# Sample attention in four 32-column groups, keys and values in one request, raw tiles without a gate

## The reference, cut to what matters

```python
def nsa_sample(pt, p, slopes, kv_pool, l, page_table, win_buf):
    ...
    raw = kv_pool[l, page_table, :, 0:2].reshape(B, past, 2, G, D)
    ...
    kc = compress(raw[:, :, :, 0], p, 0)          # gelu(blocks of 32 rows @ phi_w1 + b1) @ phi_w2
    vc = compress(raw[:, :, :, 1], p, 1)
    o_cmp, p_cmp = cmp_attend(q, kc, vc, qpos, slopes)
    idx, valid = select_blocks(p_cmp, qpos, total) # the 16 best blocks of 64 keys
    ...
    o_slc = jax.vmap(sel_attend_item, ...)(q, kb, vb, kpos, valid, qpos, slopes)
    ...
    o_win = band_attend(q[:, None], kw[:, None], vw[:, None], qpos[None], kpos_w, slopes)[:, 0]
    y = nsa_merge(pt, o_cmp, o_slc, o_win)
```

## Time and profile before

| | |
|---|---|
| median of 3 runs | 1739.01 us (1738.19 to 1742.09) |
| the profiled execution | 1731.13 us |
| its span, first to last instruction | 1729.0 us |
| TensorE busy | 1400.6 us, 81% |
| VectorE, ScalarE, GpSimd busy | 42%, 28%, 14% |
| DMA, mean | 123 GB/s |
| K/V requests `kv` | 512 of 64 KB, median 2.5 us to landing |
| window requests `rw` | 8 of 512 KB, 4.3 us |
| raw requests `rawc` and `ring` | 128 + 112 of 128 KB from GpSimd, 16 from SyncE |

### The profile page before, as it was taken

One profiled execution on the slowest core, in us unless ns is written; L12 is line 12 of the kernel. 1 busy time (PEld: TensorE's weight loads), 2 busy tenths in 40 slices (PEclk: granted clock), 3 DMA queues, 4 the chain that ended last, 5 costly groups with the idle time before them and its releaser, 6 DMA issues. The chain is left out here.

```text
span 1729.0 us, 23641 instructions
## 1 busy us (share of the span) xinstructions
PE 1400.6 (81%) x7435; PEld 1013.8 (59%) x7435; DVE 721.8 (42%) x1899; ACT 482.8 (28%) x1078; POOL 240.6 (14%) x365
## 2 busy tenths in 40 slices
PE   6899941774699478999999996797988639999991
PEld 4799940343566355677666763497878424455440
DVE  4634445443466225545565444256504621111115
ACT  2000023310155246545565452100320211111112
POOL 1000002000100242244332400000000031111112
PEclk9899985585599768999999988689987869999996
DMA  5234357102000584676566733211132536556524
GB/s 161 49 85 85 78 187 300 40 1 90 0 2 1 124 201 100 152 184 156 142 157 149 165 85 91 81 49 49 62 134 80 207 117 246 218 212 242 200 91 161
DMA packets 210114, 213.33 MB, mean 123 GB/s; under 512 B 82232, under 2 KB 179496, under 8 KB 203144
## 3 DMA queue, kind: packets, MB, share of 16 engines
q1 hardware_dynamic: 185192, 150.25, 29.1%
q0 software_dynamic: 24832, 61.94, 12.4%
HBM read 215.16 MB, written 39.37 MB: 147 GB/s over the span
## 5 line engine op out<-in xcount | busy, mean ns | idle before, releaser
L2664 PE MATMUL bank<-wgu,memtok 128*128 128x512 f32 x384 | 170.4, 597 | 1.8 <-DVE memtok L2867 1.8
L1865 ACT ACTIVATE ZTs<-bank 64x256 f32<-64x256 f32 x320 | 120.6, 377 | 86.3 <-PE bank L1724 82.2
L2664 PEld LDWEIGHTS bank<-wgu,memtok 128*128 128x128 f32 x384 | 73.5, 192 | 94.0 <-issue 94.0
L1227 PE MATMUL bank<-ZTs,w1s 128*128 128x256 f32 x512 | 114.5, 385 | 6.3 <-ACT ZTs L1865 6.3
L1227 PEld LDWEIGHTS bank<-ZTs,w1s 128*128 128x128 f32 x512 | 98.0, 193 | 26.3 <-ACT ZTs L1865 13.0
L1657 DVE COPY ZTs<-bank 64x256 f32<-64x256 f32 x192 | 80.6, 420 | 62.4 <-PE bank L1724 60.3
L1599 POOL DMA_DIRECT2D rawc<-in_cache_nsa_kv x128 | 75.2, 588 | 212.0 <-PE bank L1778 189.0
L257 PE MATMUL bank<-h_high,w_low 128*128 128x272 f32 x384 | 82.0, 295 | 9.1 <-DVE h_low L367 5.1
L2686 PE MATMUL bank<-wdn,yT 128*128 128x512 f32 x192 | 86.5, 593 | 1.5 <-DVE yT L2872 0.9
L1778 PE MATMUL bank<-KTb,QB 128*32 128x512 f32 x144 | 76.5, 615 | 6.6 <-ACT KTb L1894 5.9
L257 PE MATMUL bank<-h_high,w_high 128*128 128x272 f32 x384 | 80.9, 293 | 0.0
(11 more groups left out here) (564 smaller groups left out, 2622.0 us busy)
## 6 DMA issues: line engine op xcount, KB each, us to landing
kv<-in_cache_nsa_kv SPq DMA_DIRECT2D x512, 64.0 KB, 2.5
wgu<-in_exp_w_gate SPq DMA_DIRECT2D x24, 1024.0 KB, 5.0
wgu<-in_exp_w_up SPq DMA_DIRECT2D x24, 1024.0 KB, 7.2
wdn<-in_exp_w_down SPq DMA_DIRECT2D x24, 1024.0 KB, 4.9
rawc<-in_cache_nsa_kv POOLq DMA_DIRECT2D x128, 128.0 KB, 4.2
ring<-in_cache_nsa_kv POOLq DMA_DIRECT2D x112, 128.0 KB, 4.5
rows_dram<-ring POOLq DMA_DIRECT2D x24, 512.0 KB, 12.7
ring<-in_w_in SPq DMA_DIRECT2D x44, 256.0 KB, 3.3
```

The source lines that it names most:

```text
L1227: mm = pe.matmul(dst[:, 2 * nblk * kv:2 * nblk * (kv + 1)], w1[kv][:, c, :], ZT[:, kv, c, :, :].rearrange("p g n -> p (g n)"), start=(c == ...
L1865: return act.activation(dst, src, ACT.Copy)
L2664: mm = pe.matmul(gemm_big[n % 2][:, :].rearrange("p (m f) -> p m f", m=2), XT[:, n % 2, k, :], w[:, :, k, :], start=(k == 0), stop=(k == K ...
```

## The change

The 32 query rows used to fill 32 of the 128 rows of a bank, and 32 of the 128 columns of TensorE. Now four matmuls stand in a row whose results go to rows 0, 32, 64 and 96 (`group(j)`), each with a quarter of the keys or of the value rows. What follows from it:

- `KTb` holds four times 512 keys. Scores are taken in three places of a sequence instead of nine: the window after the first keys (4 x 128 columns), half of the past after step 5, the rest after step 8 (4 x 512 columns each).
- The tables `past`, `masked` and `bwin`, the scores `ss` and `sw` have 128 rows and a quarter of the columns. The mask is added to the table ahead (`mask_table`), and VectorE takes sum and maximum of each half in one instruction.
- Each group has its own maximum; `parts` and `scales` bring the four together, and the fold in `turn_out` (a matmul with the table `fold`) adds the four partial outputs.
- The probabilities are turned by 12 transposes of 128 x 128 or less instead of 39; two of the three banks are copied by VectorE, the last by ScalarE.
- The hidden layer is cut in two halves around the transposes of the probabilities.
- K and V of a block come in one request of 128 KB (`load_kv`), after the values of the sequence before have been taken from the block. The condition on the scores in GpSimd's requests is gone.

```diff
-            KTb = t7("KTb", [P, 2, 512])
-            PTs, PT0 = t7("PTs", [P, 2, 8 * R]), t7("PT0", [P, 3 * R])
+            KTb = t7("KTb", [P, 4, 512])
+            PTs, PT0 = t7("PTs", [P, 2, 512]), t7("PT0", [P, 7 * R])
...
-                return range(AHEAD + 3 * n // 2, AHEAD + 3 * (n + 1) // 2)
+                return range(AHEAD + 12 * (n - 2) // 7, AHEAD + 12 * (n - 1) // 7)
...
-                        for j in range(CT):
-                            sp.wait_ge(kt_mm, b * NKT + (j // 2 + 1))
-                            load_one(j, page, 0, k_here[j // 2])
...
+                    def load_kv(b):
+                        page = page_numbers(SP, b, 0) + page_numbers(SP, b, CT // 2)
+                        sp.wait_ge(o_mm, b * NO + 1)
+                        sp.dma_start(rw[:, :, :, :], I["state_nsa_win"][0, bass.ds(b, 1)].rearrange(
+                            "b (c p) v g d -> p (b c) v (g d)", p=P)).then_inc(rw_here, 16)
+                        for j in range(CT):
+                            sp.wait_ge(o_mm, b * NO + (2 + j // 4))
+                            for half in range(2):
+                                page_half(sp, kv[:, j, :, :, :], page[2 * j + half], half, slice(2, 4)).then_inc(kv_here[j // 2], 16)
...
-                        load_raw(pool, POOL, lambda j: rawc_here[j], b + 2, early, b * CT + CT, b * NKT + NKT)
+                        load_raw(pool, POOL, lambda j: rawc_here[j], b + 2, early, b * CT + CT)
...
+                    def scores(b, h):
+                        pe.wait_ge(kt_out, b * NKT + 5 + 4 * h)
+                        if h:
+                            pe.wait_ge(sl_out, b * 3 + 1)
+                        for j in range(4):
+                            mm = pe.matmul(gemm_big[h][group(j), :], QB[:, b, :], KTb[:, j, :], start=True, stop=True)
+                        mm.then_inc(sl_mm, 1)
...
+                    def values(b, h, u):
...
+                        for a in range(2):
+                            for j in range(4):
+                                at = P * (2 * u + a) + R * j
+                                mm = pe.matmul(o_at(0, group(j)), PTs[:, h, at:at + R], kv[:, 8 * h + 4 * u + j, a, 1, :],
+                                               start=(h + u + a == 0 and j > 0), stop=(h + u + a == 3))
                         mm.then_inc(o_mm, 1)
...
+                        window_scores(b)
+                        for n in range(2, NKT):
+                            keys(b, n)
+                            if more:
+                                turn_raw(b + 1, with_step(n))
+                            if n == 3 and b:
+                                turn_out(b - 1)
+                            if n == 5:
+                                scores(b, 0)
+                        scores(b, 1)
                         if more:
-                            hide(b + 1)
...
+                            hide(b + 1, 0)
+                        turn_new(b)
                         turn(b, 0)
                         turn(b, 1)
...
+                        if more:
+                            hide(b + 1, 1)
+                        values_new(b)
+                        values(b, 0, 0)
                         if more:
                             compressed_keys(b + 1)
+                        values(b, 0, 1)
+                        turn_raw(b + 2, ahead[0:1])
                         if more:
                             compressed_scores(b + 1)
+                        values(b, 1, 0)
+                        turn_raw(b + 2, ahead[1:2])
+                        values(b, 1, 1)
                         if more:
                             importance(b + 1)
+                        turn_raw(b + 2, ahead[2:4])
                         if more:
                             keys(b + 1, 0)
                             keys(b + 1, 1)
```

More of the change, by code:

```diff
@@ new lines, in turn, with values_new @@
+                    def turn(b, h):
+                        bank_ = (work[1], gemm_big[0])[h]
+                        for i in range(4):
+                            mm = pe.transpose(bank_[:, P * i:P * i + P], ss[:, h, P * i:P * i + P], ident)
+                        mm.then_inc(pt_mm, 1)
+                    def values_new(b):
+                        pe.wait_ge(pt_out, b * 2 + 1)
+                        for i in range(4):
+                            pe.matmul(o_at(1, group(i)), PT0[:, R * i:R * i + R], rw[:, i, 1, :],
+                                      start=True, stop=(i > 0))
+                        pe.matmul(o_at(1, group(0)), PT0[0:TS, P + 2 * R:P + 3 * R], vnew[:, 1, :],
+                                  start=False, stop=True)
+                        pe.matmul(o_at(2, group(0)), PT0[:, P:P + R], vc[:, :], start=True, stop=True)
+                        pe.matmul(o_at(0, group(0)), PT0[0:TS, P + R:P + 2 * R], vnew[:, 0, :],
+                                  start=True, stop=False).then_inc(o_mm, 1)
@@ new lines, in parts @@
+                    def parts(b):
+                        dve.wait_ge(e_ready, b * 2 + 2)
+                        c.step(dve.tensor_tensor(gm[0:R, 6:8], gm[0:R, 6:8], st[:, 6:8], ALU.add))
+                        for j in range(4):
+                            ins = dve.tensor_copy(pile[:, j, :], gm[group(j), 4:8])
+                        c.step(ins)
+                        c.step(dve.tensor_reduce(pile2[:, 0:2], pile[:, :, 0:2].rearrange("p j s -> p s j"), AX, ALU.max))
+                        dve.tensor_tensor(part[:, :, :], pile[:, :, 0:2],
+                                          pile2[:, 0:2].unsqueeze(1).to_broadcast([R, 4, 2]), ALU.subtract)\
+                            .then_inc(part_sub, 1)
@@ L2049, in _ @@
-                        dve.tensor_scalar(st[:, 4:5], st[:, 13:14], -1.0, None, ALU.mult).then_inc(m_ready, 1)
-                        scales(b)
+                        ahead = range(AHEAD) if b + 2 < NB else ()
+                        window_out(b)
+                        for n in range(2, NKT):
+                            if more:
+                                copy_z(dve.tensor_copy, dve, b + 1, with_step(n), 1)
+                            if n == 2 and b:
+                                merge(b - 1)
+                            if n == 3:
+                                mask_table()
+                            if n == 5:
+                                if b:
+                                    place(b - 1)
+                                scores_out(b, 0)
@@ L2051, in _ @@
+                        scores_out(b, 1)
+                        maxima(b)
+                        parts(b)
                         turned(b, 0)
                         turned(b, 1)
-                        turned(b, 2)
+                        scales(b)
                         if more:
                             compressed_scores(b + 1)
-                        turned(b, 3)
-                        turned(b, 4)
-                        if b + 2 < NB:
-                            copy_z(dve.tensor_copy, dve, b + 2, range(AHEAD), 1)
@@ L2060, in _ @@
-                        if more:
                             normalize(b + 1)
-                        turned(b, 5)
+                        copy_z(dve.tensor_copy, dve, b + 2, ahead, 1)
                         if more:
```

345 lines of the change are left out of this document (158 added, 187 removed).

## The result

The changed kernel takes 1679.11 us (median of 4 runs, 1676.70 to 1689.35) against 1740.0 for the kernel before on the same chip: a ratio of 0.966, 95% interval 0.962 to 0.970. The forecast was 1723 with a range of 1688 to 1762, so the kernel is 44 us faster than forecast, and outside the range. The profiled execution took 1676.7 us with a span of 1674.7 (before 1731.13 and 1729.0); it was the fastest of the four.

A forecast was written before the change was run, and what follows sets the result against it. TensorE's order was taken as the bound. First sequence to 702, six periods (339 us) to 1041, last period and tail to 1086, against 1101.8 before: -16 us, so 1715 profiled and 1723 as median, range 1688 to 1762.

The forecast's parts named there:

- What bounded the kernel before: Sample attention: TensorE's order was the bound, busy 52.56 of 54.3 us a sequence, with SyncE close behind at 47.7.
- TensorE's work and the column groups: Scores and values: four column groups cost one matmul; 23.9 us removed, 6.9 added, net -17 us a sequence.
- (a) SyncE: Key and value requests: 32 a sequence instead of 64, 0.72 us each, about 23 us, so SyncE stops being a bound.
- (b) DMA: Transfers up to the last keys: 8.0 MB at 250 GB/s take 32 us, so the last keys turn at about 33.
- the zero: The end of a sequence's window values, from which the forecast counted each period.
- Six periods: 6 x 56.5: Steady sequences: six periods of 56.5 us each against 54.3 before, 339 us in all, reaching 1041.
- The clock: Keys' stretch at half clock, 18.5 us or 20 with waits; 2.0 us more in the first half of the hidden layer.
- First sequence: From the first score at 658.2, 20 + 4.7 + 9 + 8.5 + 1.2 us, so its window values end at 702.
- Last sequence and tail: Last period without raw tiles or hidden layer 38.5 us, to 1079.5; value steps, merge and turn 6 us, to 1086.
- Rival 2: Keys' stretch: the clock stays at 1.0, periods of 51 us, end at 1040, -62 us, 1677; chance 0.13.
- Rival 1: K/V loading between values and next keys binds at 225 GB/s: periods of 62 us, 1756; chance 0.29.
- Rival 3: Scores and values: column groups run one behind the other, some +15 us a period, 1816; chance 0.06.

The follow-up runs named there:

- e5: The kernel before with only the gate (raw requests waiting for the scores) removed: 1736.47 us.
- e3: The changed kernel with keys and values asked for apart again, 64 requests of 64 KB a sequence: 1727.08 us.
- e4: The changed kernel with all scores and values in one row group, so no matmuls run side by side: 1727.1 us.
- e2: The changed kernel with one more 512-wide matmul, its result unused, behind each of the seven key groups of a sequence: 1692.85 us.
- e7: The changed kernel with window values and the first two value groups moved ahead of the second hidden half: 1656.01 us, ratio 0.952.
- e8: The changed kernel with half the raw bytes, in as many requests, from the third sequence on: 1661.84 us.
- e1: The changed kernel with GpSimd's first raw tile of the next but one sequence waiting for all scores again: 1697.49 us.
- e6: The kernel before with keys and values in one request, asked for after the values: 1742.39 us, ratio 1.001.

## Why the prediction was wrong, step by step

**What bounded the kernel before: half right.** TensorE's order set the five middle intervals, and removing the gate alone changed nothing (e5). But the prediction put SyncE at 47.7 us a sequence. It had left out the 11.0 us between the sequences, and with them SyncE's cycle is 59 to 61 us. So "TensorE's order is the bound" does not hold for the last two sequences: column groups alone took 8.3 us off the stage (e3), not seven times some 17. The sum of the forecast does not rest on this, since it builds the changed kernel up from its own terms.

**TensorE's work and the column groups: right.** A group of four costs one matmul, 1.07 us against 1.05, and 3.62 when it is made serial (e4). The Trainium skill (TensorE: Matmul & The Clock Gate, Part 3) has three column tiles at 2.38 times the rate of one. By that rule a group of four would cost visibly more than one matmul. No run has three; for four the trace does not agree: from start to start a group takes 0.99 us (666.75 to 667.74, full clock) against 0.98 for one matmul. Busy time in a middle sequence fell from 52.56 to 43.17 us, not by 17; in the last full period, at full clock throughout, it was 37.17, so 15.4 less, and most of the difference is matmuls at half clock.

**(a) SyncE: right for the changed kernel.** 32 requests in 23.73 us at 0.74; with 64 of them it is the bound (e3).

**(b) DMA: right for the middle sequences. The first failed step is that their transfers were charged to all six periods.** The last keys' transposes began at 32.4 us after the zero at 745.8, where 33 was forecast, with 7.6 MB moved at 234 GB/s in place of 8.0 at 250. In the first and the fifth period they began at 30.1 and 30.0 (windows at 245 and 237 GB/s), and in the sixth at 27.0, since no raw tiles are left to load. The prediction's step "Six periods: 6 x 56.5" used the middle one's transfers for all six. Against its 37.7 us from the zero to the hidden layer, the six take 34.7, 37.2, 37.1, 36.7, 34.2 and 30.3: 16 us less in all, 7.4 of them in the sixth. This is the largest single part of the error.

**The clock: the second failed step.** The prediction costed "the keys' stretch at half clock" and "first half of the hidden layer 7.0 + 2.0 for the clock". The clock did fall in the keys' stretch, but in parts: 0.50 from 756.5 to 764, 0.97 to 774, 0.56 to 781. It was full again when the hidden layer began, and both halves took 7.17 and 7.07, in this sequence and in the others. From the hidden layer's start to the zero it takes 16.8 us, not 18.7: 1.9 in each of seven, some 13 us in all.

What brings the clock back? Not the wide score groups as such. At its first return it was full from 764.5 on, 4.3 us ahead of the score group at 768.76, behind nothing but transposes and the small fold of `turn_out`:

```profile
761.50:764.50 3.00, 3.00 (x15) 2.91 (x16) 1.89 (x4) 1.73 (x4) 0.54 (x1) 0.50 1.13 248
764.50:768.70 4.20, 2.77 (x20) 2.05 (x20) 1.69 (x4) 4.08 (x14) 2.99 (x6) 1.00 1.11 232
```

At the second it rose at about 781.6, early in the score group of 781.33; in the sequences before and after this one it was full at 727.0 and 832.8, ahead of the score groups at 727.34 and 835.20. Each time TensorE had just worked through late keys and raw tiles with hardly a pause. Before the change, in rows 9, its transposes stood apart: busy 16.49 of 23.60 us from 604 to 627.6, at 0.50 all the way. What decides it was not isolated here. What the low clock cost inside the keys' stretch is not shown either: TensorE was waiting for keys much of the time, and e2 warmed it but added work.

**First sequence: 702 forecast, 694.3 measured.** 1.9 us are the hidden layer's. The rest lies in the keys' stretch: it took 19.5 us (658.07 to 677.58), not 24.7. The "20 + 4.7" had counted the last raw tiles and a score group twice, once in the 19 groups and 1.9 us of scores and once behind the last keys, and had them cold. The 20 alone would have been 0.5 us off.

**Last sequence and tail: right.** 38.5 + 6 forecast, 38.4 and 5.4 measured. That part of the gain was in the forecast, though not that 88.2 us before were so long because of SyncE; what hid it was the 2.2 us a sequence that the steady ones were to lose and did not.

The differences add up: first zero 7.7, six periods 28.1 (the 16 above, about 12 from the hidden layer), last period and tail 0.7, the rest of the program 1.6, in all 38 us, which is 1715 less 1676.7. The other 6 us lie in the step from one execution to the median: I added 8 us, and the changed kernel's median lies 2.4 above its profiled execution.

**The rivals.** Rival 2 gave 1677 us and the zero of sequence 0 at 695, and both came true, but only half of its mechanism did: the clock was full in the hidden halves, not in the keys' stretch, and its end of 1040 was 9 us too early. Taken from the profiled execution its 62 us give 1669, not 1676.7; that its 1677 lies 2 us from the median is in part luck. Rival 1 was wrong in its price: with 1 KB rows the two queues together moved 229 to 245 GB/s, and its 225 was for 512-byte rows. What it names was there, though: the K/V loading does bind the steady sequences, at 54 us and not at 62. e7 shows this from one side (the requests earlier, 47.6) and e8 from the other (fewer bytes, 48.2 to 49.7). Rival 3 was wrong. With the Trainium skill's statement that all queues share the same 16 DMA engines (Trainium Kernel Development and Optimization, Key Constraints) the trace agrees: 1.08 to 1.10 busy with both queues. But the conclusion that I hung on it, that earlier raw requests buy nothing, does not follow: e1 lost 11.9 us in the stage with the gate back, with the same bytes moved at another time: sixteen raw requests then went out beside the first keys, and the copies of the raw tiles piled up behind them.

**Which part made the gain.** Stage lengths: before 474.0; column groups without the merged request 465.7 (e3); merged request without the column groups 481.7 (in the old order, e6) and 463.9 (in the new, e4); all together 421.4. e3 and e4 keep nearly every other edit of the change, and still give only 8 and 10 us of the 52.6. TensorE at 52.6 us a sequence and SyncE at 59 to 61 with its page numbers stood so close that taking down one uncovers the other.

## What to carry to other kernels

When two resources stand close to each other, as here 52.6 and about 60 us, a change that relieves one can be worth little and a change that relieves both much; price the pair, not the parts. Read a queue's cycle from one sequence to the next, with the holes in it, and not as requests times the cost of one: a queue that began ahead can be the slower one and show it only at the end. Look for what is idle while the new bound is full: here the DMA engines stood almost still for 14 us in a middle sequence behind 32 full ones, and moving the last readers of the slots ahead of a long block of other work gave 23 us more without removing any. Sum a pipeline period by period, with its own transfers for the first, the middle and the last ones, and look up in the trace where the clock comes back before charging a low clock to what follows.

## What the runs showed of the hardware that I had not expected

- Four column groups of f32 matmuls (128x512 into 32 rows each) took 1.07 us together, against 3.62 in one group (e4) and 1.05 for a single one.
- The granted clock came back to full within the keys' stretch while TensorE was busy only 5.92 of 10.00 us (764 to 774: 0.97), and stood at 0.50 with 5.49 of 7.50 just before. The step lies at 764.5, ahead of the first score group at 768.76; from 761.5 to 764.5 TensorE was busy 3.00 of 3.00 us.
- 128 KB requests in 1 KB rows cost SyncE as much to issue (0.74 us) as 64 KB requests in 512-byte rows did before (23.87 / 32 = 0.75), and as in e3 (0.74).
- GpSimd shows 5.06 us of issue time between two sets of raw requests (e1, at 754.12), where it reads the 16 page numbers of the next eight tiles. SyncE, which reads 32, shows 11.0 us without a request between two sequences, in the kernel before and in e3. That the reading is what takes the time is inferred from the program's order; the trace doesn't list it.
